# Scores of cached keys as products and sums on VectorE and GpSimd in place of transposes and matmuls on TensorE

## The reference

```
kv = jnp.concatenate([buf, jnp.stack([k, v], axis=2).astype(buf.dtype)], axis=1)
cidx = wb + jnp.arange(T)[:, None] - dil * jnp.arange(nk)[None, :]
g = kv[:, jnp.maximum(cidx, 0)]
s = jnp.einsum('bthe,btjhe->bthj', q, g[:, :, :, 0], preferred_element_type=jnp.float32)
p = jnp.exp(s - lse[..., None])
o = jnp.einsum('bthj,btjhe->bthe', p, g[:, :, :, 1].astype(jnp.float32))
```

## Time and profile before

| what | value |
|---|---|
| median of three runs | 911.55 us |
| profiled execution | 910.62 us |
| its span, first to last instruction | 908.8 us |
| granted TensorE clock over the span | 1.0 (2.4 GHz) |
| TensorE busy | 99% |
| VectorE, ScalarE, GpSimd busy | 66%, 53%, 24% |
| gate B, slots 0 to 7 | 521.96 to 565.61 us |
| branch B's projection, 16 slots | 565.61 to 642.15 us |
| gate A, 8 slots | 642.15 to 675.51 us |

### The profile page before, as it was taken

How to read it: one execution, slowest core, us unless ns; L and a number is a source line. 1 busy time by engine, 2 the same in 40 slices (tenths; PEclk the granted TensorE clock), 3 DMA queues, 4 the chain that set the end, 5 groups by cost and what they waited for, 6 DMA issues and landing times.

```text
span 908.8 us, 19528 instructions
## 1 busy us (share of the span) xinstructions
PE 901.9 (99%) x7987; PEld 869.6 (96%) x7987; DVE 600.8 (66%) x870; ACT 485.5 (53%) x746; POOL 217.1 (24%) x233
## 2 busy tenths in 40 slices
PE   9999999999999999999999999999999999999998
PEld 8999999999999999999999999789999999999998
DVE  6666665559975688898887544455558666666543
ACT  6444434445545677677866455346655644443332
POOL 0433330005720000059871113000001043333000
PEclk9999999999999999999999999999999999999999
DMA  9988969999887877889988687859999799998971
GB/s 353 411 311 301 324 226 338 325 386 358 321 314 262 324 255 264 293 312 407 416 324 284 235 267 252 288 177 351 335 362 364 259 342 383 365 371 289 358 216 48
DMA packets 62440, 281.18 MB, mean 309 GB/s; under 512 B 8176, under 2 KB 9328, under 8 KB 60624
## 3 DMA queue, kind: packets, MB, share of 16 engines
q1 hardware_dynamic: 23328, 148.32, 42.8%
q10 hardware_dynamic: 39024, 131.61, 42.1%
HBM read 256.65 MB, written 111.32 MB: 405 GB/s over the span
## 4 chain that ended last, share of the span: by engine, by line
PE 89%; DVE 6%; DMA 2%; issue 1%; ACT 1%; SPq 0%; ACTq 0%; POOL 0%; DVEq 0%; POOLq 0%
PE acc L446 15%; PE acc L447 14%; PE acc L448 14%; PE att L446 10%; PE att L447 10%; PE att L448 10%; DVE wl L426 2%; PE aux L1085 2%; DMA raw<-w 2%; PE att L1210 1%; PE att L1144 1%; PE aux L2002 1%; PE aux L1049 1%; DMA kv<-cache 1%; PE att L827 1%
## 5 line engine op out<-in xcount | busy, mean ns | idle before, releaser
L426 DVE TENSOR_TENSOR wl<-raw,wh 128x1024 fp32r<-128x1024 f32 (+2 forms) x278 | 332.2, 1196 | 219.3 <-ACT wh L420 214.5
L420 ACT ACTIVATE wh<-raw 128x1024 fp32r<-128x1024 f32 (+2 forms) x278 | 275.2, 994 | 185.6 <-PE acc L448 104.2
L446 PE MATMUL acc<-hh,wh 128*128 128x264 f32 x496 | 145.8, 294 | 0.1
L447 PE MATMUL acc<-hl,wh 128*128 128x264 f32 x496 | 140.8, 284 | 0.0
L448 PE MATMUL acc<-hh,wl 128*128 128x264 f32 x496 | 140.6, 284 | 0.0
L446 PE MATMUL att<-xh,wh 128*128 128x264 f32 x416 | 118.6, 285 | 0.6 <-DVE xl L554 0.3
L446 PE MATMUL acc<-xh,wh 128*128 128x264 f32 x416 | 118.8, 286 | 0.0
L447 PE MATMUL att<-xl,wh 128*128 128x264 f32 x416 | 117.9, 283 | 0.0
L448 PE MATMUL acc<-xh,wl 128*128 128x264 f32 x416 | 117.8, 283 | 0.0
L447 PE MATMUL acc<-xl,wh 128*128 128x264 f32 x416 | 117.8, 283 | 0.0
L448 PE MATMUL att<-xh,wl 128*128 128x264 f32 x416 | 117.8, 283 | 0.0
(11 more groups left out here) (264 smaller groups left out, 2078.6 us busy)
## 6 DMA issues: line engine op xcount, KB each, us to landing
raw<-w ACTq DMA_DIRECT2D x207, 512.0 KB, 7.0
state<-state_in SPq DMA_DIRECT2D x32, 512.0 KB, 9.2
state_out<-state SPq DMA_DIRECT2D x32, 512.0 KB, 6.2
raw<-w ACTq DMA_DIRECT2D x32, 384.0 KB, 5.8
kv<-cache SPq DMA_DIRECT2D x48, 256.0 KB, 4.5
raw<-w ACTq DMA_DIRECT2D x32, 320.0 KB, 5.7
raw<-w SPq DMA_DIRECT2D x9, 512.0 KB, 8.7
kv_out<-cache SPq DMA_DIRECT2D x3, 960.0 KB, 7.2
```

The lines of the kernel that those rows point to most:

```text
L420: nc.scalar.activation(wh[n % HI_RING][:, 0:slot_size(n)], raw[n % RAW_RING][:, 0:slot_size(n)], ACT.Copy).then_inc(hi_done, 1)
L426: nc.vector.tensor_tensor(wl[n % RAW_RING][:, 0:slot_size(n)], raw[n % RAW_RING][:, 0:slot_size(n)], wh[n % HI_RING][:, 0:slot_size(n)].bi ...
L446: nc.tensor.matmul(out, w_hi, xh, start=first, stop=False)
L447: nc.tensor.matmul(out, w_hi, xl, start=False, stop=False)
```

## The change

- **Scores.** Queries of the samples are packed by GpSimd (`pool_pack`) and transposed once by TensorE (`pe_q_rows`, four transposes at the end of the v phase) into `bank6`, where 32 rows a quarter hold one query per sample, group and half. The cached keys stay with rows on partitions. They come in six items (3 groups x 2 sets of four samples), each of two buffers of 128x2x512. For each item VectorE spreads the query rows over the partitions (`dve_key_spread`, a shuffle of 128x512), multiplies (`dve_key_product` for the first three items, the query in PSUM; `pool_key_product` for the last three, the query in SBUF, each half as two operations of 128x512), and VectorE sums over the 64 elements of a head (`dve_key_sum`, 1024 columns to 16). No key transposes, copies, score matmuls or clearing are left. Own scores are 48 small matmuls against GpSimd's products.
- **Softmax** in two sets of four samples (`dve_soft_max`, `act_soft_exp`, `dve_soft_sum`), VectorE's block transpose and shuffles joining the groups. Each set has its own turn, value matmuls (three items of 4 matmuls) and gather (`pe_dec_gather`, 8 matmuls).
- **Places.** The tables by slot number u (-8 to -1 gate B, 0 to 15 `p_pb`, 16 to 23 `p_ga`) say where each step stands. On VectorE they stand before the attention's steps of that slot.
- **Loads.** 12 key loads of 512 KB, 48 value loads of 32 partitions, 128 KB each; an item waits until the item three before it has been summed or multiplied.
- **Other.** ScalarE's and GpSimd's split of branch B is one slot later and TensorE waits for it by quarter; both turned halves of the prompt's probabilities share `bank5`; the sample columns of branch A's output are split last, in one step, and `p_pa` waits for all splits before its first matmul. Tables and buffers are laid out anew.

```diff
         def pe_turn(pe, i, r):
             pe.wait_ge(att_prob, 2 * i + r + 1)
-            if i:
-                pe.wait_ge(att_copied[r], i)
-            elif r == 0:
-                pe.wait_ge(v_own_done, 1)
+            if r:
+                pe.wait_ge(att_copied[0], i + 1)
+            elif i:
+                pe.wait_ge(att_copied[1], i)
             for n in range(4):
-                last = nc.tensor.transpose(turn_bank(r)[:, n * P:(n + 1) * P], prob[:, r, n * P:(n + 1) * P], ident)
...
+        def kv_used(sp, n):
+            if n < ITEMS:
+                sp.wait_ge(key_sum, 2 * n + 2)
+            else:
+                sp.wait_ge(dec_v_done, n - ITEMS + 1)
+        def kv_landed(n):
+            return sum(32 if m < ITEMS else 128 for m in range(n % 3, n + 1, 3))
+        def sp_kv_load(sp, n):
+            if n >= 3:
+                kv_used(sp, n - 3)
+            c, g = n % ITEMS // G, n % G
+            dil = GROUPS[g][1]
+            for half in range(2):
+                buffer = kv_buffer(n, half)
+                if n < ITEMS:
+                    rows = caches[g][4 * c:4 * c + 4].rearrange("b w c -> (b w) c").rearrange(
+                        "(p k d) c -> p k d c", k=4, d=dil)
+                    sp.dma_start(buffer[:], rows[:, 2 * half:2 * half + 2, 0, 0:AW]).then_inc(kv_in[n % 3], 16)
+                else:
+                    two = caches[g][4 * c + 2 * half:4 * c + 2 * half + 2].rearrange("b (p k d) c -> k p b d c", k=4, d=dil)
+                    for k in range(4):
+                        sp.dma_start(buffer[32 * k:32 * k + 32], two[k, :, :, 0, AW:2 * AW]).then_inc(kv_in[n % 3], 16)
+        def pool_pack(pool):
+            nc.gpsimd.memset(q_pack[:], 0.0).then_inc(q_packed, 1)
+            pool.wait_ge(q_packed, 1)
             pool.wait_ge(qks_done, 1)
+            nc.gpsimd.memset(scoreT[:], 0.0).then_inc(q_packed, 1)
+            for g in range(G):
+                to = q_pack[:].rearrange("p n (j i) -> p n j i", j=4)[:, :, :, 2 * g:2 * g + 2]
...
+        def pe_q_rows(pe):
+            pe.wait_ge(q_packed, 2 + G)
+            pe.wait_ge(state_new, 2 * STATES)
+            for n in range(4):
+                last = nc.tensor.transpose(bank6[:, n * P:(n + 1) * P], q_pack[:, n], ident)
+            last.then_inc(q_rows, 1)
...
+            pe.wait_ge(q_packed, 3 + G)
+            for t in range(AT):
+                a = 2 * (AT - 1 - t)
+                for j in range(4):
+                    last = nc.tensor.matmul(bank7[32 * j:32 * j + 32, 0:2], head[:, a:a + 32], own_prod[:, t, j:B:4],
+                                            start=t == 0, stop=t == AT - 1)
+            last.then_inc(own_scored, 1)
...
+        def spread_to(i):
+            return att4[:, i % 2] if i < G else q_wide[:]
+        def dve_key_spread(dve, i):
+            if i == 0:
+                dve.wait_ge(q_rows, 1)
+            if i >= 2:
+                dve.wait_ge(key_mul, 2 * i - (2 if i == 2 else 0))
+            c, g = i // G, i % G
+            nc.vector.stream_shuffle(spread_to(i), bank6[:], [2 * g + c] * 32).then_inc(key_spread, 1)
+        def dve_key_product(dve, i, half):
+            dve.wait_ge(kv_in[i % 3], kv_landed(i))
+            dve.wait_ge(key_spread, i + 1)
+            if i or half:
+                dve.wait_ge(key_mul, 2 * i + half)
+            keys = kv_buffer(i, half)
+            nc.vector.tensor_tensor(keys[:], keys[:], spread_to(i).unsqueeze(1).to_broadcast([P, 2, AW]),
+                                    ALU.mult).then_inc(key_mul, 1)
+        def pool_key_product(pool, i, half):
+            pool.wait_ge(kv_in[i % 3], kv_landed(i))
+            pool.wait_ge(key_spread, i + 1)
+            pool.wait_ge(key_mul, 2 * i + half)
+            keys = kv_buffer(i, half)
+            nc.gpsimd.tensor_tensor(keys[:, 0], keys[:, 0], spread_to(i), ALU.mult)
+            nc.gpsimd.tensor_tensor(keys[:, 1], keys[:, 1], spread_to(i), ALU.mult).then_inc(key_mul, 1)
+        def dve_key_sum(dve, i, half):
+            dve.wait_ge(key_mul, 2 * i + half + 1)
+            if i == 0:
+                dve.wait_ge(q_packed, 2)
+            if i == G and half == 0:
+                dve.wait_ge(soft_step, 1)
+            g = i % G
+            to = scoreT[:].rearrange("p (k x) -> p k x", k=4)[:, 2 * half:2 * half + 2, AH * g:AH * g + AH]
+            nc.vector.tensor_reduce(to, kv_buffer(i, half)[:].rearrange("p k (h e) -> p k h e", h=AH), AX.X,
+                                    ALU.add).then_inc(key_sum, 1)
...
+        def dve_soft_max(dve, c):
+            dve.wait_ge(key_sum, 2 * G * (c + 1))
+            nc.vector.transpose(pR[:, c, 0:P], scoreT[:]).then_inc(soft_step, 1)
+            if c == 0:
+                dve.wait_ge(own_scored, 1)
+            nc.vector.tensor_copy(pR[:, c, P:P + 1], bank7[:, c:c + 1] if c == 0 else dec_m[:, 1, 7:8]).then_inc(soft_step, 1)
+            if c == 0:
+                nc.vector.tensor_copy(dec_m[:, 1, 7:8], bank7[:, 1:2]).then_inc(soft_step, 1)
...
+        def pe_dec_turn(pe, c):
+            pe.wait_ge(dec_dve, 2 * c + 2)
+            if c:
+                pe.wait_ge(dec_out, 2)
+            nc.tensor.transpose(bank7[:, P:2 * P], pR[:, c, 0:P], ident)
+            rsel = TABLES["rsel"][0]
+            nc.tensor.matmul(bank7[0:32 * G, 2 * P:2 * P + 4 * AH], tab[:, rsel + 4 - 4 * c:rsel + 4 - 4 * c + 32 * G],
+                             dec_diag[:], start=True, stop=True).then_inc(dec_pe, 1)
...
+        def pe_dec_gather(pe, c):
+            pe.wait_ge(v_own_done, c + 1)
+            pe.wait_ge(vs_out, AT)
+            for n in range(4):
+                nc.tensor.matmul(bank7[:, 8 * n:8 * n + 8], v_s[:, n * P:(n + 1) * P],
+                                 dec_own[0:32 * G, c, 8 * n:8 * n + 8], start=n == 0, stop=False, skip_group_check=True)
+            for n in range(4):
+                last = nc.tensor.matmul(bank7[:, 8 * n:8 * n + 8], v_own[:, n * P:(n + 1) * P],
+                                        const("own_seq"), start=False, stop=n == 3, skip_group_check=True)
+            last.then_inc(dec_gathered, 1)
...
+        DEC_TURN = {6: 0, 15: 1}
+        DEC_V = {9: (0,), 11: (1,), 12: (2,), 17: (3, 4), 18: (5,)}
+        DEC_GATHER = {14: 0, 20: 1}
+        KEY_SPREAD = {-8: 0, -7: 1, -2: 2, 1: 3, 4: 4, 7: 5}
+        KEY_PRODUCT = {-8: (0,), -6: (1,), -4: (2,), -3: (3,), -2: (4,), 0: (5,)}
+        KEY_SUM = {-6: (0,), -5: (1,), -4: (2,), -3: (3,), -1: (4,), 1: (5,), 6: (6, 7), 8: (8, 9), 10: (10, 11)}
+        SOFT_MAX = {2: 0, 11: 1}
+        SOFT_EXP = {3: 0, 12: 1}
+        SOFT_SUM = {4: 0, 13: 1}
+        OWN_ROWS = {13: 0, 19: 1}
+        DEC_OUT = {14: 0, 20: 1}
...
+                if t == KD - 2:
+                    act.wait_ge(dec_out, 4)
+                    nc.scalar.activation(oah[:, :, S:T], oa[:, :, S:T], ACT.Copy).then_inc(oa_hi, 1)
...
+            for i in range(G, ITEMS):
+                for half in range(2):
+                    pool_key_product(pool, i, half)
...
-                for n in range(3):
-                    steps[3].append(lambda n=n: pe_key_turn(pe, 3 * t + n))
-                if t == 0:
-                    steps[3] += [small_sum, lambda: pe_score_clear(pe)]
-                else:
-                    for n in range(3):
-                        steps[3].append(lambda n=n: pe_key_score(pe, 3 * t - 3 + n))
+                if t == 1:
+                    steps[3] += [small_sum, lambda: pe_own_score(pe)]
                 pe_wide_half(pe, p_gb, t // 4, t % 4, between=steps)
...
+                dec = steps[3 if second else 2]
+                if u in DEC_TURN:
+                    dec.append(lambda: pe_dec_turn(pe, DEC_TURN[u]))
+                for n in DEC_V.get(u, ()):
+                    dec.append(lambda n=n: pe_dec_v(pe, n))
+                if u in DEC_GATHER:
+                    dec.append(lambda: pe_dec_gather(pe, DEC_GATHER[u]))
...
-                        if m == 0:
-                            pe.wait_ge(oa_split, k + 1)
+                        if m == 0 and k == 0:
+                            pe.wait_ge(oa_split, 5)
```

More of the change, by code:

```diff
@@ new lines, in pe_dec_v @@
+        def pe_dec_v(pe, i):
+            c, g = i // G, i % G
+            if g == 0:
+                pe.wait_ge(dec_act, 2 * c + 2)
+            n = ITEMS + i
+            pe.wait_ge(kv_in[n % 3], kv_landed(n))
+            for j in range(4):
+                a = 32 * j + AH * g
+                last = nc.tensor.matmul(bank7[32 * j:32 * j + 32, :], dec_pT[:, a:a + 32], kv_buffer(n, j // 2)[:, j % 2],
+                                        start=g == 0, stop=g == G - 1)
+            last.then_inc(dec_v_done, 1)
@@ L1257, in pool_blocks, with dve_dec_out @@
+        def dve_dec_out(dve, c):
+            dve.wait_ge(dec_gathered, c + 1)
             for r in range(2):
                 rows = slice(r * AE, (r + 1) * AE)
[L1259 to L1262 removed]
@@ L1283, in key_copy @@
-        def key_copy(eng, i):
-            eng.wait_ge(key_turned, i + 1)
```

(54 more changed lines are left out.)

327 lines of the change are left out of this document (142 added, 185 removed).

## The result

The changed kernel takes 922.2 us (median of four runs, 919.52 to 923.17) against 911.53 of the kernel before (911.03 to 912.01): a ratio of 1.0112, interval 1.0098 to 1.0127. It is slower by 1.1%, where 902.5 was forecast. The profiled execution took 921.63 us beside 910.62.

A forecast was written before the change was run, and what follows sets the result against it. TensorE, busy 99% of the span, was taken as the bound. Profiled 910.6 - 16.65 of work + 7.6 of stalls = 901.6, and 0.9 for the median gave 902.5 us; forecast 897 to 907, wider range 895 to 910.

The forecast's parts named there:

- The work on TensorE: Samples' matmuls and transposes: 22.65 us removed, 6.0 us added, net -16.65 us.
- VectorE's and GpSimd's prices: New steps: products 1.2 us, sums 1.2 (up to 2.0), spreads 0.7 on VectorE; GpSimd products 1.35, upper bound 3.2.
- Gate B has no stall: Gate B: VectorE falls up to 3.5 us behind, 5.5 us of lag are covered, so TensorE does not wait.
- the prompt cache rolls ... start some four slots later and have until the last phase: SyncE's rolls behind the value loads start at u = 12 instead of 8; no cost was given.
- Slots 6 and 7: Two sums between split and reciprocal at u = 6 make TensorE wait 1.9 us in slot 7.
- slot 8: The wait carried over from slot 7 and a spread at u = 7 cost 0.7 us here.
- Slot 12: TensorE waits 3.1 us (1.5 to 5) for the third value item, loaded only after the sums at u = 10.
- Slots 9 and 11: Sums at u = 8 and 10 make TensorE wait 1.1 us in slot 9 and 0.5 us from u = 10.
- Sample columns last: Before branch A's projection TensorE waits for all splits; a small split behind the fourth costs 0.3 us.
- A slower kernel: Rival: GpSimd products at 4.3 us each hold up the spread, scores and splits; 914.5 us, chance 0.06.
- The cover holds: Rival: VectorE and SyncE come in time everywhere; 894.9 us, chance 0.2.
- The second rival: VectorE or the loads become the bound for a dozen slots; 909.5 us at most, chance 0.2.

The follow-up runs named there:

- the combination: Changed kernel with 4 KB roll packets, VectorE's attention steps ahead of sample steps, softmax before the spread in slot 4, third value item in slot 13: 896.2 us, ratio 0.9821.
- e5_roll_packets: Changed kernel with the prompt cache rolls moved in 4 KB packets instead of 64 KB, same bytes and places: 905.9 us, ratio 0.9939.

## Why the prediction was wrong

- **The work on TensorE: right.** Forecast -16.65 us. Summed from start to start, and with the waits under 0.4 us, which the forecast also counted, all matmuls but the weights' take 64.9 us before and 48.4 in the combination, from the v phase to branch A's projection: -16.5. (In slot 14, at the lower clock described at the end, they take 0.8 us more than in the changed kernel.) The phases themselves are 14.5 us shorter, with the v phase's 0.4 for the query transposes; the other 2.0 are waits and slower matmuls that were not there before: 1.3 at the end of slot -6 for ScalarE's gate, 0.7 in slot 1 for GpSimd's split of branch B.
- **VectorE's and GpSimd's prices: right.** Sums forecast at 1.2 us, products 1.2, GpSimd's 1.35, spread 0.7. Measured, by shape (busy us, mean ns) and by tile (ns min/median/max):

```profile
L1327 DVE TENSOR_REDUCE scoreT<-kv 128x16 f32<-128x1024 f32 x12 | 14.3, 1209 | 0.1
L1306 DVE TENSOR_TENSOR kv<-kv,att 128x1024 f32<-128x1024 f32 x6 | 7.3, 1213 | 0.2
...
L1316 POOL TENSOR_TENSOR kv<-kv,q_wide x6: 1278/1796/2359, 557.8 to 586.0; 128x512 f32<-128x512 f32 x6
```

  GpSimd took 1.28 us alone and up to 2.4 behind a VectorE split. The spread took 0.69 to 0.74. The warning against `tensor_reduce` that the prediction cites did not come true at this shape: a sum took 1209 ns, a product of as many columns 1213.
- **Gate B has no stall: nearly.** Its last four slots take 2.90 us each where they took 5.21; the wait of 1.3 in slot -6 is the only one.
- **The step that failed: "the prompt cache rolls ... start some four slots later and have until the last phase".** The rolls had the time; what was not asked is what they do to the queue beside them. Priced at nothing, they cost in slots 22 to 24 a stretch of 24.7 us where the combination needs 10.3: 14.4 us, of which 11.5 are idle time of TensorE. In e5_roll_packets, where the packets alone are changed, these slots take 10.3 too. The earlier trace rows priced the landing of the samples' own loads; the landing of the weights beside the rolls was not read at all.
- **The clock: missing in the sum.** After the gaps TensorE ran slower:

```profile
612.00:618.00 6.00, 6.00 (x41) 4.94 (x38) 0.00 (x0) 1.50 (x3) 0.00 (x0) 0.63 1.04 234
...
670.00:675.00 5.00, 0.00 (x0) 0.00 (x0) 0.00 (x0) 0.00 (x0) 0.00 (x0) 0.60 1.05 356
675.00:680.00 5.00, 1.70 (x8) 1.73 (x9) 1.23 (x1) 1.51 (x3) 0.00 (x0) 0.50 0.74 235
680.00:685.00 5.00, 2.96 (x19) 2.79 (x19) 1.98 (x4) 2.98 (x6) 0.00 (x0) 0.84 0.99 391
685.00:690.00 5.00, 5.00 (x30) 5.00 (x31) 1.36 (x3) 0.00 (x0) 0.00 (x0) 0.69 1.40 587
```

  From 612 to 618 us TensorE is busy all the time and its clock is 0.63 of full, so for most of the stretch at the lower level, 1.2 GHz for 2.4. Beyond idle time this cost 3.0 us in slots 22 to 24 (14.4 - 11.5), 1.7 in slots 6 and 7 (15.2 less 4.9 idle, against 8.6 busy in the combination) and 2.6 in slot 12 (11.6 against 8.7 in e5_roll_packets, where the gap is 0.3 shorter and the clock stays at 1.00): 7.3 us in all.
- **Slots 6 and 7: right in place and releaser, too small.** Forecast 1.9 us in slot 7; together they lost 6.4 against the combination. The 2.4 us of sums were there, but the split ahead of them ended 6.4 us after slot 6 began (575.6 - 569.2) and not 3.2, since VectorE came out of slot 4 three us late: its spread was followed by a softmax that took 4.2 us instead of 1.2, shut out by GpSimd's products. The prediction had no term for slot 4, took the overlap as 0.2 us a split and looked only at splits. In slot 8 there was no wait (4.51 us).
- **Slot 12: the wait was right, the clock behind it was missing.** Forecast 5.6 + 9.5 - 12.0 = 3.1. Slot 10 began at 595.5 us, the loads were issued from 601.3 (5.8 later), the last landed at 610.8 (9.5 later), and TensorE stood ready at 607.4 (11.9 after the slot's start): it waited 3.4, and the slow clock brought the loss to about 6.
- **Slots 9 and 11: right.** Forecast 1.1 and 0.5. TensorE waited 0.73 and 0.29 us before the turns for ScalarE's scaling, and the slots are 0.8 and 0.4 longer than in the combination.
- **Sample columns last: right,** 0.3 us, hidden in the combination (branch A's projection 12.29 us for 12.21).
- **The rivals.** A slower kernel was given a chance of 0.06, and on another ground: the loss was put on GpSimd's products at 4.3 us. They took 1.3 to 2.4, and the loss had another cause. "The cover holds" gave 894.9, and the kernel with the four edits takes 896.2. (The second rival's terms give 910.6 - 16.65 + 14.9 + 0.9 = 909.8, not 909.5, and the forecast's range begins once at 899 and once at 897; nothing hangs on either.)

The sum with the measured terms: 910.6 - 16.5 (work) + 2.0 (what the combination loses more than before) + 14.4 (slots 22 to 24) + 6.4 (6 and 7) + 3.8 (12 to 14, less than slot 12's own 6 because the combination pays 2.2 for the moved item) + 1.2 (9 and 11) = 921.9, the profiled execution being 921.6.

## What to carry to other kernels

When a change delays an engine that issues transfers, list what comes due meanwhile: it is issued in one burst, and its harm can be in the landing of other queues' transfers, not in its own. Beside a stream of small loads that must be on time, shape bulk copies into packets of the same size, and repair that first, since a late stream takes back what is gained ahead of it. Price a wait of a few microseconds on TensorE with the slower matmuls behind it, and look at what runs on GpSimd beside each small VectorE step on the way to TensorE.

## What the runs showed of the hardware

- **The size of packets on one queue sets the share of another.** With 64 KB packets on one queue and 4 KB on another, halves of 512 KB landed in 29.0 us at the median; with 4 KB on both, in 8.4, at nearly the same total of bytes. With the large ones an engine passed 1.7 weight packets for each of a roll.
- **Loads of 128 KB into 32 partitions are slower per byte** than loads of 512 KB into 128: 0.137 against 0.095 us for a 2 KB packet. Width and size of the load changed together, and which part of the path limits them was not tried.
- **A one-column VectorE step can take five times as long:** 1.24, 1.08 and 1.37 us for 0.22, 0.29 and 0.24, each until a GpSimd multiply ends. The Trainium skill (SBUF — State Buffer, "Who interferes with whom") has a VectorE instruction with two SBUF inputs excluded by a GpSimd one that reads SBUF. The first of the three steps, with two input columns, agrees. The other two have one input besides a scalar per partition and are held up as well, while the multiplication of a column by a constant took 0.15 us beside a product. Whether the scalar or the way of reading 129 and 32 columns makes the difference was not separated.

```profile
571.54 0.15 DVE L1159 TENSOR_SCALAR att_m<-att_m 128x1 f32<-128x1 f32 x1
...
569.69 2.36 POOL L1316 TENSOR_TENSOR kv<-kv,q_wide 128x512 f32<-128x512 f32 x1
```

- **The clock can fall without a gap.** In the combination's slot 14 no idle time is over 0.4 us, TensorE is busy 8.04 of 8.41 us with value, gather and attention matmuls, and its clock is 0.80; the slot takes 2.2 us longer than in the changed kernel (6.21). The three other kernels with a value item in slot 13 show the same clock and length. What triggers it stays open.

```profile
607.83:613.64 5.81, 5.81 (x51) 4.49 (x49) 3.88 (x14) 2.07 (x4) 0.00 (x0) 1.00 1.06 244
613.64:622.05 8.41, 8.04 (x62) 7.48 (x61) 3.36 (x10) 3.67 (x7) 0.00 (x0) 0.80 1.04 263
```
